# Token-wise post-norms, later column sums and three reordered stretches in a two-block transformer kernel on one core

## The reference

```python
def rmsnorm(x, gain):
    y = x32 * lax.rsqrt(jnp.mean(x32 * x32, axis=-1, keepdims=True) + RMS_EPS)
    return (y * gain.astype(jnp.float32)).astype(x.dtype)
...
    # first block: the output of each part is normed too ("post-norm"), then added
    h = token_mixer(rmsnorm(x, norm_mix_pre[l]), ...)
    x = x + rmsnorm(h, norm_mix_post[l])
    h = memory_cross_attention(rmsnorm(x, norm_cross_pre[l]), rmsnorm(mem, mem_norm[l]), ...)
    x = x + rmsnorm(h, norm_cross_post[l])
    h = conv_glu_ffn(rmsnorm(x, norm_ffn_pre[l]), ...)
    x = x + rmsnorm(h, norm_ffn_post[l])
...
    # second recurrence: gates, then attention with decays, then an output gate
    f_gate = lb + (1.0 - lb) * jax.nn.sigmoid(z); log_f = jnp.log(f_gate)
    k_h = 1.0 - f_gate; q_h = jax.nn.silu(...)
    y_h = head_rmsnorm(o_h, hgrn_norm) * jax.nn.silu(h_g.astype(f32))
...
    # second block: norms only ahead of a part; odd layer per head
    yn = (yf - mu) * lax.rsqrt(var + GN_EPS) * gn_g
    return (jax.nn.silu(g) * yn) @ w_out
```

## Time and profile before

| what | value |
|---|---|
| time, median of 3 runs | 2315.23 us (2314.81 to 2315.4) |
| the profiled execution's own time | 2315.41 us |
| its span, first to last instruction | 2313.6 us |
| mean granted TensorE clock | 0.976 of full speed |
| busy: PE, ACT, DVE, POOL | 95%, 37%, 45%, 35% |

### The profile page before, as it was taken

How to read it: one execution, slowest core, us unless ns; L and a number is a source line. 1 busy time by engine, 2 the same in 40 slices (tenths; PEclk the granted TensorE clock), 3 DMA queues, 4 the chain that set the end, 5 groups by cost and what they waited for, 6 DMA issues and landing times.

```text
span 2313.6 us, 26996 instructions
## 1 busy us (share of the span) xinstructions
PE 2187.5 (95%) x9972; PEld 1724.4 (75%) x9972; DVE 1042.4 (45%) x1528; ACT 854.1 (37%) x1275; POOL 815.4 (35%) x343
## 2 busy tenths in 40 slices
PE   6889998989999988998999999999999988999999
PEld 5766676758888865765788888788878766888887
DVE  5556646485534363357432312335742665322121
ACT  5334544432222242446442322435432433433231
POOL 3322224224444432220344444443333323444443
PEclk9899999989999999999999999999999999999999
DMA  4212112113322341110222322322222212323223
GB/s 148 66 53 74 64 64 91 64 54 106 123 95 96 100 136 55 64 46 1 83 98 93 100 93 98 107 91 72 75 68 81 80 46 73 97 95 100 95 97 101
DMA packets 54967, 193.36 MB, mean 84 GB/s; under 512 B 6096, under 2 KB 6352, under 8 KB 54480
## 3 DMA queue, kind: packets, MB, share of 16 engines
q1 hardware_dynamic: 50400, 181.58, 24.0%
q10 hardware_dynamic: 4464, 10.36, 1.4%
HBM read 189.82 MB, written 2.10 MB: 83 GB/s over the span
## 4 chain that ended last, share of the span: by engine, by line
PE 73%; issue 13%; DVE 9%; POOL 3%; ACT 2%; DMA 0%; POOLq 0%; SPq 0%; DVEq 0%; ACTq 0%
PE gemm_ps L500 22%; PE gemm_ps L501 21%; PE gemm_ps L502 21%; POOL wl L469 3%; PE out_ps L908 2%; DVE tmp L1654 1%; DVE arena L2022 1%; DVE tmp L2029 1%; PE turn_ps L695 1%; DVE arena L1654 1%; PE score_ps L686 1%; DVE x L1676 1%; PE out_ps L705 1%; DVE xl L1654 1%; PE score_ps L900 1%
## 5 line engine op out<-in xcount | busy, mean ns | idle before, releaser
L469 POOL TENSOR_TENSOR wl<-raw,wh 128x1024 fp32r<-128x1024 f32 x339 | 815.2, 2406 | 1480.4 <-ACT wh L1137 1480.3
L500 PE MATMUL gemm_ps<-xh,wh 128*128 128x512 f32 x1512 | 612.9, 405 | 44.2 <-DVE xl L1654 24.8
L1137 ACT ACTIVATE wh<-raw 128x1024 fp32r<-128x1024 f32 x339 | 359.0, 1059 | 774.5 <-DMA raw<-w_in 745.6
L501 PE MATMUL gemm_ps<-xl,wh 128*128 128x512 f32 x1512 | 593.3, 392 | 0.0
L502 PE MATMUL gemm_ps<-xh,wl 128*128 128x512 f32 x1512 | 593.3, 392 | 0.0
L501 PE MATMUL gemm_ps<-arena_r,wh 128*128 128x512 f32 (+1 forms) x1124 | 433.0, 385 | 0.0
L500 PEld LDWEIGHTS gemm_ps<-xh,wh 128*128 128x128 f32 x1512 | 286.9, 190 | 125.7 <-issue 46.9
L500 PE MATMUL gemm_ps<-arena_r,wh 128*128 128x512 f32 (+1 forms) x868 | 335.5, 387 | 10.8 <-DVE arena_r L1659 10.1
L501 PEld LDWEIGHTS gemm_ps<-xl,wh 128*128 128x128 f32 x1512 | 287.2, 190 | 65.5 <-issue 7.9
L502 PE MATMUL gemm_ps<-arena_r,wl 128*128 128x512 f32 (+1 forms) x868 | 333.3, 384 | 0.0
L502 PEld LDWEIGHTS gemm_ps<-xh,wl 128*128 128x128 f32 x1512 | 286.5, 189 | 61.0
(11 more groups left out here) (334 smaller groups left out, 2011.1 us busy)
## 6 DMA issues: line engine op xcount, KB each, us to landing
raw<-w_in SPq DMA_DIRECT2D x339, 512.0 KB, 3.3
arena<-na_in ACTq DMA_DIRECT2D x14, 256.0 KB, 2.7
x<-x_in SPq DMA_DIRECT2D x8, 256.0 KB, 6.6
out<-x ACTq DMA_DIRECT2D x8, 256.0 KB, 2.8
arena<-alibi_in ACTq DMA_DIRECT2D x6, 256.0 KB, 3.3
con<-con_in SPq DMA_DIRECT2D x1, 1432.0 KB, 11.9
arena<-moba_in ACTq DMA_DIRECT2D x1, 1024.0 KB, 5.1
arena<-mem_in ACTq DMA_DIRECT2D x1, 1024.0 KB, 4.8
```

The source lines that it names most:

```text
L469: pool.tensor_tensor(wl[:, k, :], raw[:, k, :], wh[:, k, :].bitcast(F32), ALU.subtract).then_inc(unit_split, 1)
L500: pe.matmul(o, wh[:, n % RING, w], h[:, kt, 0:width], start=(kt == 0), stop=False)
L501: pe.matmul(o, wh[:, n % RING, w], l[:, kt, 0:width], start=False, stop=False)
L1137: act.activation(wh[:, k % RING, :], raw[:, k % RING, :], ACT.Copy).then_inc(high_split, 1)
```

## The change

It has five parts.

1. The three post-norms work on a column per 128 tokens. `token_norm` multiplies the squares (as the stationary operand) with a single column of ones, so that the sums come out as 128x4; ACT's root and DVE's reciprocal are over 128x4; and PE spreads the result over the partitions again with four products of a broadcast column and the identity (`spread_rstd`, in PSUM), which `add_normed` reads. PE waits in `token_norm` for the reciprocal.
2. Behind the mixers and the cross attention ACT squares the last block (the last two) from PSUM, without waiting for DVE's copy (`direct`, `banks`, `half_crossed`); behind the mixers `memory_scaled(b)` comes after `add_normed(b)` and no longer one ahead of it.
3. Three pre-norms (ahead of both MLPs and of the retention) add all eight squares on DVE and make one sum on PE (`whole_sum`), issued inside the next unit, behind its 6th of 8 input blocks (`after=`).
4. In the second recurrence forget gates, `edges` and `far_operands(0)` are made before the output gate's units are taken; the output gate is opened later, in `mlstm`; `FILL_START` goes from 3 to 1 and level 6 gets a fill unit in both pairs; the wait for `weights_used` moves behind the first factors of the second pair.
5. The last heads' units are dealt out otherwise (`HEAD_STEPS`): two units of head 7 take the place of head 6's gates, and head 7's gates come behind its retention has begun; the output units begin at steps 3 and 4.

```diff
+HEAD_STEPS = [[(h, u) for u in range(U_HEAD)] for h in range(RH - 2)]
+HEAD_STEPS.append([(RH - 2, 0), (RH - 2, 1), (RH - 2, 2), (RH - 2, 3), (RH - 1, 0), (RH - 1, 1)])
+HEAD_STEPS.append([(RH - 1, 2), (RH - 1, 3), (RH - 2, 4), (RH - 2, 5)])
+HEAD_STEPS.append([(RH - 1, 4), (RH - 1, 5)])
-FILL_START, FILL_LEVELS = 3, (0, 1, 2, 3, 4, 5)
+FILL_START, FILL_LEVELS = 1, (0, 1, 2, 3, 4, 5, 6)
...
+                    if after is not None and kt == nkt - 3:
+                        after()
...
+            def whole_sum():
+                take(square_added, KT - 1)
+                pe.matmul(turn_ps[:, 0, :], ones, square_sum, start=True, stop=True).then_inc(square_used, 2)
+            def token_sums(squares, first, last):
+                for c in range(T):
+                    col = CCOL["col"] + 4 - c
+                    m = pe.matmul(turn_ps[:, 0, 0:T], squares[:, c * P:(c + 1) * P], con[:, col:col + T],
+                                  start=(first and c == 0), stop=(last and c == T - 1), skip_group_check=True)
+                return m
+            def token_norm(apart=1):
+                take(square_added, KT - 1 - apart)
+                token_sums(square_sum, True, False)
+                if apart == 2:
+                    take(square_made, KT - 1)
+                    token_sums(sq[:, (KT - 2) % 2, :], False, False)
+                take(square_made, 1 if apart == 2 else KT)
+                token_sums(sq[:, (KT - 1) % 2, :], False, True).then_inc(square_used, 2)
+                take(token_rstd_ready)
+                for c in range(T):
+                    m = pe.matmul(spread_rstd[:, c * P:(c + 1) * P], token_rstd[:, c:c + 1].broadcast_to([P, P]),
+                                  ident, start=True, stop=True)
+                m.then_inc(rstd_spread, 1)
...
-            added_sum()
-            units(FIRST["mup0"], 1, mh, ml, fresh=True)
+            units(FIRST["mup0"], 1, mh, ml, fresh=True, after=whole_sum)
...
             for s in range(U_HEAD):
+                if s < 2:
+                    unit(ret_unit(*HEAD_STEPS[RH][s]), xh, xl)
                 retention(RH - 1, s)
-                for n, at, first, end in ((out1, 0, 0, 6), (out1 + 1, 3, 0, 2), (out1 + 1, 4, 2, 6)):
+                for n, at, first, end in ((out1, 3, 0, 6), (out1 + 1, 4, 0, 6)):
...
+            def inverse_tokens():
+                take(std_ready)
+                done(dve.reciprocal(token_rstd, token_std), token_rstd_ready)
+                take(rstd_spread)
...
-                stt(tmp[:, b % 2, :], y[:, b, :], p_(post, b), rstd[:, :], ALU.mult, ALU.mult)
+                stt(tmp[:, b % 2, :], y[:, b, :], p_(post, b), spread_rstd, ALU.mult, ALU.mult)
...
-                    if b:
-                        take(weights_used)
...
+                            if b and lev == 1:
+                                take(weights_used)
                             scores(lev - 1)
...
             for b in range(KT):
-                if b < 7:
-                    memory_scaled(b + 1)
                 add_normed("norm_mix_post", "norm_cross_pre", b)
+                memory_scaled(b)
```

213 lines of the change are left out of this document (128 added, 85 removed).

## The result

| | before | changed |
|---|---|---|
| time, median | 2315.32 us (2314.81 to 2315.69, 4 runs) | 2276.46 us (2275.06 to 2276.74, 4 runs) |
| ratio | | 0.983, 95% interval 0.9814 to 0.9846 |
| span of the profiled execution | 2313.6 us | 2275.0 us |
| PE busy | 2187.5 us | 2175.7 us |

The account below looks back on a forecast made before the run. PE was taken as the bound, busy 2187.5 of 2313.6 us, with waits that also lower its clock. Terms 5.0 + 6.6 + 1.6 + 6.6 + 2.8 + 6.5 + 6.2 + 4.5 = 39.8 gave 2275.5 us, range 2265 to 2288.

Parts of the forecast that it names:

- Start of the recurrence: Second recurrence's preparation: two units moved elsewhere, scans and keys ahead of gate rows, `far` starting near 81.3; saves 5.0 us.
- Value 5.0: Saving put on preparing the second recurrence; 2 if ACT's copies in between come late, 6 at most.
- if the first level waits for ACT: Second recurrence, first level: a sign that would show the prediction wrong; no size given.
- Level 6 and the second pair: Second recurrence: a unit covers last-level waits of 1.64, other waits and a slow stretch shrink; 6.6 plus 1.6 us saved.
- Norm behind the cross attention: Post-norm there: last products to first feed-forward product falls from 14.9 to 8.3 us, saving 6.6.
- Norm behind the feed-forward: Post-norm there: small root and reciprocal, two token sums, less 1.04 of spreading; saves 2.8 us, bounds 2.2 and 3.3.
- Norm behind the mixers: Post-norm there: DVE's first block 5.7 us earlier, last column sum 5.7 to 7.6 earlier; saves 6.5.
- PE's own pace is then quicker than what it did: Memory units behind the mixers: PE had waited for squares; taking `memory_scaled` one step later breaks that circle; no separate size.
- Pre-norms: Three pre-norms: unit starts at once with one sum inside, no 1.36 wait; saves 6.2 us, bounds 4 and 7.
- last heads: Head 6's squares to the output unit's product: shorter than 46.5 us; saves 4.5, bounds 0 and 7.
- Waits did take places of the removed ones: Rival, whole kernel: steps moved forward delay neighbours, only 24.6 us saved, 2291 us; chance 0.20.
- The clock was kept in part: Rival, stretches behind the norms: they stay at 2.4 GHz, perhaps 10 to 15 us more, 2263 us; chance 0.08.

Follow-up runs that it names:

- the wide norm: Changed kernel with the three post-norms' sum of squares spread over all partitions again, root and reciprocal over 512 columns: 2285.1 us, ratio 0.9882.

## Why the prediction was right, and where not

*Start of the recurrence: 5.0 predicted, 2.4 measured.* The step that failed is "Value 5.0": the text named the lower end, 2, for the case that ACT's copies come late, and chose a value near the upper, 6. It had followed `far(0)`'s operands through the new order (76 said, 77.2 measured) and the clearing and the taking of a unit on DVE ("ends at about 82.7"; 83.15), but stopped there. The differences, the exponent and three copies still stood behind them, in one chain across DVE and ACT, and `far(1)` waited for its end. So `far(0)` came 4.6 us earlier, the two moved units aside, nearly as predicted, and 2.3 of that was lost again ahead of `far(1)`, where the wait grew from 1.72 to 3.99. The list of signs had "if the first level waits for ACT"; it did, for 1.02, but it had done so for 1.02 before the change too.

*Level 6 and the second pair: 8.2 and 7.5.* The waits of 1.64 went. New ones in the first pair are 1.02 ahead of the sixth level's scores and 0.46 ahead of the weighted products; the second trace of the changed kernel has only 0.31 of them. The difference of 0.7 is smaller than the 2.4 between these two traces of one kernel, so this term is borne out no closer than that. The clock's share (2.2) came about: where the earlier trace rows has two slow stretches at 154.6 and 161.4, one of 3.4 at 149.9 is left.

*Norm behind the cross attention: 6.6 and 6.5.* Its pieces hold too: 3.4 for direct squares, 2.3 for the small root and reciprocal. The 24 instructions of token sums took 2.73 us, 114 ns each. By the Trainium skill's floor of 25 ns between matmuls (TensorE: Matmul & The Clock Gate, Wait — 56ns, not 53.3ns?) this term would have been 8.4. The trace keeps to the floor but stands at over four times it: eight instructions with 4 columns are 0.95 us in the row above, not much less than eight with 128 columns (1.16).

*Norm behind the feed-forward: 2.8 and 2.1*, below the bound of 2.2. The mis-sized piece is the way from the reciprocal's end to DVE's first block. The sum had only the spreading there, 1.04; it took 1.67 (820.60 to 822.27), since a handoff to PE and one back, which the sum left out, stand around it.

*Norm behind the mixers: 6.5 and 9.4*, above the upper bound of 7.6. The step "PE's own pace is then quicker than what it did" was right and had no number. DVE's first block came 5.4 earlier behind the norm's start (5.7 said); from there to the first cross score it is 43.4 us instead of 47.5, and these 4.1 are the term that was missing. What went there is waiting: PE's for squares and `xl` fell from 3.2 + 2.0 us to 0.3, DVE's for the memory units from 8.4 to 3.0. DVE's own work did not get shorter (29.2 us busy before, 30.3 now). Two runs show conditions of the gain: the order of the taking (9.9 lost without it, so also all of the shift) and the factors in PSUM (4.3 lost without them in the wide norm). The second did not speed DVE up against the kernel before, since its three wide groups took 26.6 us there and 26.9 now; it kept the denser order from meeting POOL more often. No run put the new order alone into the kernel before.

*Pre-norms 6.2 and 6.5, last heads 4.5 and 3.6* were as worked out, the heads within their wide bounds of 0 to 7, with the signs named: no 1.36, 0.54 ahead of unit 2 of the retention (0.7 said), 2.00 and 2.81 behind head 6, 3.59 at the output unit.

*Rivals.* Waits did take places of the removed ones. The four kinds listed above came to 6.3 us before and to 11.7 now, so 5.4 us are new, and only at the start of the recurrence by more than a microsecond beyond what the sum held. The clock was kept in part: 11.0 us of the 38.7. The sum didn't show that, since it took stretches of before in their slow length; so the two add up to no extra. No wait for `wl` appeared.

Two errors, -2.6 and +2.9, hid each other in the total. That the total fits to about 1 us is therefore partly luck. Each was found only by laying both traces side by side.

## What to carry to other kernels

When a wait is removed by reordering, follow the chain of the next thing that PE asks for too, across all engines, to its end; a first product that starts early is worth nothing if the second stands behind the same queue. Shortening one engine's step pays only if the work that used to be hidden beside it doesn't become what is waited for: take results of later units behind, not ahead of, the block that PE needs next. Measure the stretches singly; a total that fits can be two errors. And trace the same kernel twice before a difference of 2 us in one stretch is put down to an edit.
